# Tile order of the forgetting attention reversed by halves; splits held back, a value product inside the first norm, Pool in the norms' rows

## The reference

```
for branches S5, forgetting attention, RWKV, stick-breaking attention:  y_n = branch(h @ w_in)
merged = sum_n sigmoid(gates_n) * (y_n @ w_branch_n)
h   = layer_norm(alpha * h + merged @ w_out)                 # the first norm
ffn = square(relu(h @ mlp_w1)) @ mlp_w2
ple = sigmoid(h @ ple_gate_w) * (p @ ple_w)
h   = layer_norm(alpha * h + ffn + ple)                      # the second norm

forgetting attention, head by head, query tile i of 128 rows (keys 0 .. 128*(i+1)):
    logits = q k / 8 + c_query - c_key, masked above the diagonal;  out = softmax(logits) v
stick-breaking attention, same tiles:
    z = q k / 8;  weights = exp(log_sigmoid(z) + sum of log_sigmoid(-z) over the later keys);  out = weights v
```

## Time and profile before

| | us |
|---|---|
| median of 3 runs | 3736.1 (3733.81 to 3738.7) |
| profiled execution, its own time | 3734.22 |
| its span, first to last instruction | 3732.4 |
| attention with its gates | about 2314 to 2653 |
| gated branches | 2653 to 2761 |
| w_out, the first norm | 2761 to 2843, 2843 to 2893 |
| gate product, MLP | 2893 to 3692 |
| second norm and output | 3692 to 3732.4 |

### The profile page before, as it was taken

One profiled execution on the slowest core, in us unless ns is written; L12 is line 12 of the kernel. 1 busy time (PEld: TensorE's weight loads), 2 busy tenths in 40 slices (PEclk: granted clock), 3 DMA queues, 4 the chain that ended last, 5 costly groups with the idle time before them and its releaser, 6 DMA issues. The chain is left out here.

```text
span 3732.4 us, 42191 instructions
## 1 busy us (share of the span) xinstructions
PE 3453.7 (93%) x18138; PEld 2932.2 (79%) x18138; DVE 1684.4 (45%) x1984; ACT 763.5 (20%) x1071; POOL 923.4 (25%) x532
## 2 busy tenths in 40 slices
PE   8998999999899999987985998999897999999996
PEld 7986889998688988776864996666685788888885
DVE  3235663322566351163547554555677221312136
ACT  2112331111333110000011221555423010101012
POOL 2350002335000233330223322110131233333331
PEclk9999999999999999999997998999999999999998
DMA  3120001112000133310131003220351111111111
GB/s 116 46 78 11 19 1 35 60 44 81 8 19 1 35 110 116 119 67 19 56 123 38 1 1 93 71 57 26 125 177 43 48 46 47 50 49 48 51 46 57
DMA packets 65100, 208.75 MB, mean 56 GB/s; under 512 B 9824, under 2 KB 11488, under 8 KB 64772
## 3 DMA queue, kind: packets, MB, share of 16 engines
q1 hardware_dynamic: 60452, 189.81, 15.6%
q10 hardware_dynamic: 4464, 16.25, 1.1%
HBM read 165.05 MB, written 40.37 MB: 55 GB/s over the span
## 5 line engine op out<-in xcount | busy, mean ns | idle before, releaser
L195 POOL CAST w_hi<-w_raw 128x1024 fp32r<-128x1024 f32 x195 | 218.0, 1118 | 2511.7 <-PE psum L206 1734.3
L197 POOL TENSOR_TENSOR w_lo<-w_raw,w_hi 128x1024 fp32r<-128x1024 f32 x195 | 521.4, 2674 | 15.6
L206 PE MATMUL psum<-x,w_hi 128*128 128x512 f32 x1536 | 416.2, 393 | 16.2 <-DVE x L3028 13.9
L712 PE MATMUL psum<-h,w_hi 128*128 128x512 f32 x1024 | 339.3, 414 | 43.7 <-DVE gate_stage L739 28.4
L206 PEld LDWEIGHTS psum<-x,w_hi 128*128 128x128 f32 x1536 | 288.4, 188 | 83.3 <-DVE x L3028 15.2
L712 PEld LDWEIGHTS psum<-h,w_hi 128*128 128x128 f32 x1024 | 195.3, 198 | 96.3 <-issue 30.5
L206 PE MATMUL psum<-x,w_lo 128*128 128x512 f32 x768 | 236.9, 390 | 0.0
L712 PE MATMUL psum<-h,w_lo 128*128 128x512 f32 x512 | 207.0, 404 | 0.0
L206 PE MATMUL psum<-hn_hi,w_hi 128*128 128x348 f32 x864 | 189.0, 327 | 17.8 <-DVE hn_lo L458 16.3
L206 PE MATMUL psum<-h,w_hi 128*128 128x512 f32 x736 | 197.0, 389 | 0.0
L206 PE MATMUL psum<-hn_hi,w_lo 128*128 128x348 f32 x864 | 185.1, 322 | 0.0
(11 more groups left out here) (423 smaller groups left out, 6490.1 us busy)
## 6 DMA issues: line engine op xcount, KB each, us to landing
w_raw<-in_w_mlp SPq DMA_DIRECT2D x64, 512.0 KB, 3.5
w_raw<-in_w_in SPq DMA_DIRECT2D x36, 512.0 KB, 3.5
w_raw<-in_w_gates SPq DMA_DIRECT2D x32, 512.0 KB, 3.8
gates_kept<-gate_stage SPq DMA_DIRECT2D x64, 256.0 KB, 2.1
gates<-gates_kept SPq DMA_DIRECT2D x32, 512.0 KB, 4.1
w_raw<-in_w_out SPq DMA_DIRECT2D x24, 512.0 KB, 3.6
w_raw<-in_w_branches_in SPq DMA_DIRECT2D x23, 512.0 KB, 3.5
proj_kept<-stage ACTq DMA_DIRECT2D x23, 512.0 KB, 2.6
```

The source lines that it names most:

```text
L195: self.core.nc.gpsimd.tensor_copy(self.hi[:, g % 2], self.raw[:, g % 2]).then_inc(self.hi_done, 1)
L197: self.core.nc.gpsimd.tensor_tensor(self.lo[:, g % 2], self.raw[:, g % 2], self.hi[:, g % 2].bitcast(F32), ALU.subtract) \
L206: last = nc.tensor.matmul(acc[:, c, :], w[:, g % 2, k, :], x(k)[:, c * ch:(c + 1) * ch], start=(k == 0 and part == 0), stop=(k == kt - 1 a ...
L712: last = nc.tensor.matmul(self.core.psum[:, self.bank(x // KT), :], one[:, g % 2, k, :], other(k)[:, c * CH2:(c + 1) * CH2], start=(k == 0 ...
```

## The change

- **Order of the tiles.** `tile(i)` of a forgetting step is moved by half a head: tiles 5, 6, 7, 8, 1, 2, 3, 4 of each head in place of 1 to 8. The wait for a head's queries and keys hangs on the number in the head, not on the tile.
- **Splits held back.** `Weights.split` can wait between the cast and the subtraction. It does so for three tiles: the second tile of the gated branches (until four lower parts of y are done), the second of w_out (until all eight lower parts of the merged rows are done), the second of the per-layer gate (until the norm's squares are all added).
- **Order in the gated branches.** ACT makes the upper part of a finished row after the first gate of the next tile, not the second; DVE makes the lower part ahead of the second gated product, not ahead of the fourth.
- **Value product inside the norm.** The first value product is made in two halves in `tensor_end`, one ahead of the column sums, one ahead of the spreads.
- **Pool in the rows.** In the first norm Pool makes five of the eight lower parts (rows 0, 1, 2, 4, 5). In the second norm ACT copies the second spread to SBUF and Pool does three of the eight subtractions (rows 1, 3, 5); DVE multiplies one row ahead of them.

```diff
     def tile(i):
-        return steps[i][1] % NQ2
+        return (steps[i][1] + (NQ2 // 2 if fox(i) else 0)) % NQ2
...
-                if j == 0:
+                if number(i) % NQ2 == 0:
                     pe.wait_ge(qk_in[kind][hd % 2], (48 if fox(i) else 32) * (hd // 2 + 1))
...
-    def split(self, pool, g):
+    def split(self, pool, g, between=None):
...
             self.core.nc.gpsimd.tensor_copy(self.hi[:, g % 2], self.raw[:, g % 2]).then_inc(self.hi_done, 1)
+            if between:
+                between(pool)
             pool.wait_ge(self.hi_done, g + 1)
...
-                    w.split(pool, g)
+                    w.split(pool, g, (lambda pool: pool.wait_ge(y_lo_done, 4)) if g == self.g0 + 1 else None)
...
-                    if m % 4 == 1 and m > 4:
+                    if m % 4 == 0 and m:
                         high(m // 4 - 1)
...
+                    if n == 1 and j:
+                        low(j - 1)
                     nc.vector.tensor_tensor(halves(tmp[:, use % 2, :] if n else rows(j)),
...
-                    if n == 2 and j:
-                        low(j - 1)
...
+    LOWS, SUBTRACTED = (0, 1, 2, 4, 5), (1, 3, 5)
+    def wait_sums(self, eng):
+        eng.wait_ge(self.sq_added, KT - 1)
...
+    def gpsimd(self, pool):
+        nc = self.core.nc
+        for k in self.lows:
+            pool.wait_ge(self.ready, k + 1)
+            nc.gpsimd.tensor_tensor(self.lo(k), self.x(k), self.hi(k).bitcast(F32), ALU.subtract) \
+                .then_inc(self.x_lo_pool, 1)
+        for k in self.subtracted:
+            pool.wait_ge(self.copied, 1)
+            pool.wait_ge(self.centered, self.HALF + k + 1)
+            nc.gpsimd.tensor_tensor(self.x(k), self.x(k), self.c, ALU.subtract).then_inc(self.scaled_pool, 1)
+
+    def tensor_end(self, pe, fill=None):
         nc, psum = self.core.nc, self.core.psum
+        if fill:
+            fill(pe, 0)
...
             last.then_inc(self.summed, 1)
+        if fill:
+            fill(pe, 1)
         for n in range(2):
             pe.wait_ge(self.diag, n + 1)
...
         nc.scalar.activation(self.sm[:, 1], self.sm[:, 1], ACT.Sqrt).then_inc(self.root, 1)
+        if self.subtracted:
+            act.wait_ge(self.spread, 2)
+            nc.scalar.activation(halves(self.c), self.spread_bank(1), ACT.Copy).then_inc(self.copied, 1)
         for k in range(KT):
-            act.wait_ge(self.scaled, k + 1)
+            self.wait_scaled(act, k)
...
+        dve.wait_ge(self.spread, 1)
         if self.lo:
+            for k in range(KT):
+                times(k)
+                subtract(k)
+                if k >= 1 and k - 1 not in self.lows:
+                    low(k - 1)
             low(KT - 1)
+        else:
+            multiplied = 0
+            for k in range(KT):
+                if k not in self.subtracted:
+                    while multiplied <= k + (k + 1 in self.subtracted):
+                        times(multiplied)
+                        multiplied += 1
+                    subtract(k)
...
         gemm(core, KT, hi, lo, NC2, CH2, residual, None, coming=load_h, norm=one, split=merged_lo,
-             free=lambda pe: branches.wait_gated(pe, N_GATES - 4))
+             free=lambda pe: branches.wait_gated(pe, N_GATES - 4),
+             calm=lambda pool: pool.wait_ge(merged_lo, KT), fill=ple.first_values)
+        ple.make()
```

Otherwise `gated_products` becomes a class, `GatedProducts`, so that its first value product (`values`, one half a call) can be made by `fill`; its tile 0 no longer makes one, and Pool calls `norm.gpsimd` behind its split of the second tile:

```diff
+    def first_values(self, pe, c):
+        self.values(pe, self.core.weights.taken, 0, c)
...
+                    w.split(pool, g, norm.wait_sums if g == g0 + 1 else None)
+                    if g == g0 + 1:
+                        norm.gpsimd(pool)
```

More of the change, by code:

```diff
@@ L233, in gemm @@
 def gemm(core, n, hi, lo, nch, ch, evac, src, rows=None, total=None, sq=None, coming=(), ahead=None, taken=None,
-         norm=None, split=None, free=None, heads=None):
+         norm=None, split=None, free=None, heads=None, calm=None, fill=None):
     nc, w = core.nc, core.weights
@@ L277, in _ @@
             for g in range(g0 + 1, g0 + n + 1):
-                w.split(pool, g)
+                w.split(pool, g, calm if g == g0 + 1 else None)
         @block.tensor
@@ L299, in _ @@
             if norm:
-                norm.tensor_end(pe)
+                norm.tensor_end(pe, fill)
         @block.scalar
@@ L2887 @@
 class RowNorm:
     HALF = KT // 2
+    LOWS, SUBTRACTED = (0, 1, 2, 4, 5), (1, 3, 5)
     SEMAPHORES = ("totalled", "c_summed", "c_ready", "shifted", "centered", "squared", "sq_added", "summed", "small",
-                  "root", "diag", "spread", "scaled", "ready", "x_hi", "x_lo", "stored")
+                  "root", "diag", "spread", "scaled", "ready", "x_hi", "x_lo", "x_lo_pool", "copied", "scaled_pool", "stored")
     def __init__(self, core, x, g, b, factor, buffers, ones, ident, semaphores, hi=None, lo=None, out=None):
@@ L2919, in tensor_beside, with wait_low, wait_scaled @@
             last.then_inc(self.c_summed, 1)
-    def tensor_end(self, pe):
+    def wait_sums(self, eng):
+        eng.wait_ge(self.sq_added, KT - 1)
+    def wait_low(self, eng, k):
+        if k in self.lows:
+            eng.wait_ge(self.x_lo_pool, self.lows.index(k) + 1)
+        else:
+            eng.wait_ge(self.x_lo, k + 1 - sum(n < k for n in self.lows))
+    def wait_scaled(self, eng, k):
+        if k in self.subtracted:
+            eng.wait_ge(self.scaled_pool, self.subtracted.index(k) + 1)
+        else:
+            eng.wait_ge(self.scaled, k + 1 - sum(n < k for n in self.subtracted))
+    def gpsimd(self, pool):
[9 more added lines that the diff above has]
+    def tensor_end(self, pe, fill=None):
         nc, psum = self.core.nc, self.core.psum
+        if fill:
+            fill(pe, 0)
         for n, (sem, count, rows) in enumerate(((self.totalled, KT - 2, self.total),
@@ L3044, in vector_end, with times, subtract @@
         spread(1)
-        for k in range(KT):
-            if k == 0:
-                dve.wait_ge(self.spread, 1)
+        def times(k):
             nc.vector.tensor_tensor(halves(x(k)), halves(x(k)), self.spread_bank(0), ALU.mult).then_inc(self.centered, 1)
+        def subtract(k):
             if k == 0:
                 dve.wait_ge(self.spread, 2)
+                if self.subtracted:
+                    dve.wait_ge(self.copied, 1)
             dve.wait_ge(self.centered, self.HALF + k + 1)
             nc.vector.tensor_tensor(halves(x(k)), halves(x(k)), self.spread_bank(1), ALU.subtract).then_inc(self.scaled, 1)
-            if self.lo and k >= 1:
-                low(k - 1)
+        dve.wait_ge(self.spread, 1)
         if self.lo:
-            low(KT - 1)
+            for k in range(KT):
[3 more added lines that the diff above has]
+                    low(k - 1)
+            low(KT - 1)
+        else:
+            multiplied = 0
+            for k in range(KT):
+                if k not in self.subtracted:
[3 more added lines that the diff above has]
+                    subtract(k)
     def sync(self, sp):
@@ L3137, in _ @@
             two.sync(sp)
+        @block.gpsimd
+        def _(pool):
+            two.gpsimd(pool)
 def mlp(core, h, hi, lo, hidden_hi, hidden_lo, stage, norm):
```

141 lines of the change are left out of this document (76 added, 65 removed).

## The result

The changed kernel takes **3701.18 us** (median of 4 runs, 3699.56 to 3702.61) beside 3734.95 for the kernel before (4 runs): ratio 0.9912, 95% interval 0.9895 to 0.9929. The gain of 33.8 us is larger than the 29.0 of the forecast's sum, and 3701.18 lies 5.8 us under the predicted 3707, inside the range. A second set of 4 runs gave 3702.08. The profiled execution took 3702.61 (span 3700.8, mean clock 0.971).

What follows compares the result with a forecast made beforehand. TensorE, busy 93% of the span, was taken as the bound, with time to win only where it stands still or runs below full clock. Terms 9 + 3 + 3.7 + 9.8 + 3.5 = 29.0 us gave 3707 us, range 3698 to 3719.

Steps and rivals of the forecast that it cites:

- A: Attention: the new order of the forgetting tiles saves 9 us at its end and 3 us in its body.
- the end: Attention's last 44.6 us: PE's wait for the exponential goes, other waits and half-clock time shrink; 9 us saved.
- B: Gated branches and w_out: held splits save 0.9 and 2.8 us, the moved lower half 0; sum 3.7, bounds 1 and 5.
- C: First norm: held split, value product inside the norm and Pool's five lower halves save 9.8 us, bounds 5 and 13.
- D: Second norm: three subtractions on Pool and ACT's copy of the second spread save 3.5 us, bounds 1 and 4.
- become a chain: Attention's wide pairs: PE's next scores wait for both tiles' work, 43 us more, 3753 in all; chance 0.04.
- Of the clock I give back half: Attention's last 44.6 us: of about 4.9 us lost to PE's reduced clock, 2.4 are counted as regained.
- the body's 5.5: Attention before its last 44.6 us: 5.5 us lost to clock, part of 13 us of which 3 were expected back.
- The lower half moved ahead of the second product: Gated branches: moving DVE's lower half forward adds no DVE work, stands in PE's covered part, and is worth 0.
- rival 5: Gated branches: held splits only move PE's wait from the lower half to w_lo, bringing 1 us; 3710 in all, chance 0.07.
- Rival 3: Norms: Pool and DVE block each other, lower halves of rows 3 and 6 wait; 5 us more, 3712, chance 0.13.
- Rival 4: Clock stays up through the norm's sums (4 us) and the end of attention (3 us); 3700, chance 0.13.

Runs made afterwards that it cites:

- no_fill: The changed kernel with the first value product of the next matrix back behind the norm instead of in two halves inside it: 3703.8 us, ratio 0.9922.
- no_holds: The changed kernel without Pool's three held splits, the lower half keeping its new place: 3705.9 us, ratio 0.9927.
- low_before_wait: The changed kernel with DVE's lower half of a merged tile put ahead of its wait for the next gate: 3696.97 us, ratio 0.9899.
- pool_none: The changed kernel with all lower halves and all subtractions of the two norms on DVE, none on Pool: 3712.97 us, ratio 0.9946.

## Why the prediction was nearly right, step by step

| term | forecast | measured (means over the executions in the table) |
|---|---|---|
| A, last head | 9 (called the end) | 14.5 |
| A, the rest | 3 | 4.9 |
| B, branches and product | 3.7 | -1.6 + 1.1 = -0.5 |
| C, first norm | 9.8 | 10.5 |
| D, second norm | 3.5 | 3.5 |
| sum | 29.0 | 32.9 |

The sum came out nearer than its terms: A brought 7.4 us more than forecast and B 4.2 less. That these two misses offset each other in part is luck.

- **A, right in mechanism, too small in size.** Equals beside equals did not become a chain: no wait of the scores was left in the wide pairs. The pair of 1024 keys took 11.8 us from one forgetting tile's scores to the next in the last three heads (12.4 in the first), where I had estimated 12.3. The mis-sized term is "Of the clock I give back half" (2.4, and next to nothing of the body's 5.5). Measured: busy time fell by 6.5 us in the last head and 2.4 in the other three, 8.9 in all, beside the 10.4 that the clock had cost. Idle time fell by 8.0 and 2.5, 10.5 in all, and that part I had nearly right (5.6 + 2.4 - 1.4 + 3 = 9.6). When the short waits went, nearly all of the half-clock time went with them: what is left is the 5.4 us at the end of the drain. I also drew the line between end and body too late: the order of the last head sets its whole 82.2 us and not only the last 44.6.
- **B, wrong, in one step.** "The lower half moved ahead of the second product changes no count of DVE work and stands in PE's covered part: 0" counted the instruction and not the wait it was put behind. Behind the wait for the next gate it idles DVE 1.0 us in each of seven tiles; DVE falls behind PE's 11.1 us per tile (88.7 us for eight), and PE waits at the stage's end, in some executions already earlier for a gated product (1.0 to 2.5 us). Cost against the old place: 3.5 us (111.25 against 107.8). The holds themselves were sized nearly right for the kernel they were worked out on: 3.0 us for the 3.7, with the halves at their old place. But the two edits aren't independent: with the lower half ahead of the wait the holds are worth nothing (106.1 without, 106.05 with). The number is near rival 5 (B brings 1, chance 0.07), the reason is another: that rival has the holds only move PE's wait, and at the stage's end they replaced 2.24 us by 0.79.
- **C, right in sum, not in its parts.** The held split and the fill were to bring 4.5; the mean is 4.8 (17.8 to 13.0). Most of it is the hold: 3.9 without the filling (13.95 in no_fill) and 5.3 with it (18.3 in no_holds), forecast 2.2. With the total late the column sums too run at half clock (6.99 us in no_holds, 3.73 to 5.91 with the hold). The fill brought about 1 where 2.3 was forecast: the spreads, which were to run warm in 3.4 us, took 4.30 us in the changed kernel and 4.66 in low_before_wait. Rows: 5.7 in the mean for 5.3. The changed kernel's own profile (11.5 + 27.0) was a lucky one: the same program also had 13.2.
- **D, right**: 3.5 in the mean, and 4.0 between executions whose column sums took the same time.
- **Rival 3** (Pool and DVE block each other in the norms) didn't occur in either split of the rows. The Trainium skill (page SBUF — State Buffer, section "Who interferes with whom") says that a DVE instruction with at most one SBUF input, outside the modes that use two ports, doesn't contend with Pool. The rows agree: beside Pool's 7.21 us for three lower halves DVE's multiplications and subtractions took 1.22 each. The rule of the Trainium skill's GPSIMD Engine Reference (section "Elementwise — side-by-side cycle accounting": elementwise work belongs on DVE) would have cost 9.9 us here, the 5.9 and 4.0 of pool_none: Pool's 2.36 is paid by nobody while ACT sets the pace.
- **Rival 4** (the clock stays up) is not one case but differs from execution to execution: the sums took 11.5, 13.2 or 14.8 us with the same instructions. The Trainium skill's page TensorE: Matmul & The Clock Gate (section "What's actually happening") says that the number of cold matmuls differs between runs of one kernel; these three lengths agree with it.

## What to carry to other kernels

In the attention the short waits cost their idle time (10.5 us) and, with it, nearly as much again in matmuls at half clock (8.9 us). Where a stretch shows both, price them together, and expect both back when the waits go; but read the granted clock first, for at the end of the changed kernel's branches two waits of 1.59 and 0.79 us left it at 1.00. An instruction moved forward in an in-order engine is free only if it also passes the waits ahead of it; ask of each move what the engine waits for just before. Measure two edits of one stage apart as well as together: the holds brought 3.0 us with the halves at their old place and nothing with the lower half at its best. And make the tiles that nothing stands beside the narrowest, with the narrowest of them last.

## What the runs showed of the hardware

- The same instructions of the norm's sums took 11.5, 13.2 or 14.8 us by where PE's clock fell; 32 products of one column took from 3.73 to 5.91 us there, and from 4.66 to 6.99 us in the second norm. The second norm's other length, 37.6 for 36.0, came with 6.9 to 7.0 us for them. The rows of low_before_wait there, then of the changed kernel:

```profile
3661.10 6.99 PE L2986 MATMUL psum<-ones,ln_rows 128*128 128x1 f32 x32 [2.58 <-DVE ln_rows L3029]
```
```profile
3667.31 4.92 PE L2986 MATMUL psum<-ones,ln_rows 128*128 128x1 f32 x32 [2.58 <-DVE ln_rows L3029]
```

- So a difference under some 3 us in one profiled stage with PE half idle is no finding; the attention, where PE is busy 97%, repeated within 0.3 us in ten executions.
- What stays open: why the first score moves by up to 8 us between executions though the code ahead of it is the same.
